# One-hot gate spreading in a transformer kernel: iota read from PSUM, low parts all on GpSimd, copies out of PSUM in 16-byte runs, one group of expert tiles fewer beside it

## The reference, cut to what matters

```python
idx = jnp.take_along_axis(cand_i..., best_pos, axis=-1)      # 8 heads x 16 experts per token
gate = jax.nn.softmax(best_s, axis=-1)
...
act = jax.nn.gelu(jnp.einsum('bpd,bphkd->bphk', hb, u_tab[ib]), approximate=False)
coef = (act * gb).astype(hb.dtype)
return jnp.einsum('bphk,bphkd->bpd', coef, v_tab[ib])
```

## Time and profile before

| | before |
|---|---|
| median of 3 runs | 2282.73 us (2278.05 to 2283.14) |
| profiled execution, its own time | 2281.69 us |
| span of the profiled execution | 2279.9 us |
| busy: PE, DVE, POOL, ACT | 2137.2, 1462.7, 1047.4, 926.5 us |
| mean granted clock of TensorE | 0.981 |

### The profile page before, as it was taken

The page is one execution under the profiler, slowest core; times in us unless marked ns, Lnnn a source line. Parts: engine busy times, 40 slices in busy tenths (PEclk is TensorE's granted clock), DMA queues, the critical chain, the costliest instruction groups (busy, mean ns, idle before and its releaser), DMA issues.

```text
span 2279.9 us, 27268 instructions
## 1 busy us (share of the span) xinstructions
PE 2137.2 (94%) x10296; PEld 1675.8 (74%) x10296; DVE 1462.7 (64%) x2308; ACT 926.5 (41%) x1527; POOL 1047.4 (46%) x828
## 2 busy tenths in 40 slices
PE   8999999999999999999999988787888699999999
PEld 6877767468787667878787766666666588888887
DVE  6456175442337742248989599999995366666665
ACT  4223354642333233013344466566664444433342
POOL 6555654304232217778588877777775300000000
PEclk9999999999999999999999999999999799999999
DMA  5221322202011112232166545556667688888884
GB/s 202 86 78 71 130 68 88 73 28 84 32 43 56 56 38 93 93 129 93 56 194 210 188 147 213 199 211 232 217 206 260 249 288 291 289 288 288 289 287 160
DMA packets 98291, 359.32 MB, mean 158 GB/s; under 512 B 8480, under 2 KB 41504, under 8 KB 73328
## 3 DMA queue, kind: packets, MB, share of 16 engines
q1 hardware_dynamic: 98160, 357.56, 45.4%
HBM read 286.09 MB, written 71.30 MB: 157 GB/s over the span
## 4 chain that ended last, share of the span: by engine, by line
PE 66%; DVE 18%; POOL 8%; issue 5%; ACT 3%; DMA 1%; SPq 0%; DVEq 0%; POOLq 0%; ACTq 0%
PE ps L1434 10%; PE ps L1435 10%; PE ps L797 9%; PE ps L798 9%; PE ps L799 9%; POOL wring_parts L2621 5%; DVE area L2505 2%; PE ps L1244 2%; PE ps L786 2%; PE ps L1381 2%; PE ps L1382 2%; DVE area L2489 2%; DVE area L2408 2%; DVE area L2490 2%; DVE area L2405 1%
## 5 line engine op out<-in xcount | busy, mean ns | idle before, releaser
L1381 PE MATMUL ps<-sqbuf_parts,wring_parts 128*128 128x512 f32 x1024 | 423.4, 413 | 23.7 <-POOL wring_parts L2621 23.7
L2621 POOL TENSOR_TENSOR wring_parts<-wring_parts,wring 128x512 fp32r<-128x512 f32 x256 | 380.8, 1515 | 136.9 <-ACT wring_parts L1852 136.9
L2577 POOL CAST wring_parts<-wring 128x512 fp32r<-128x512 f32 x236 | 169.6, 759 | 546.1 <-PE ps L799 429.1
L1382 PE MATMUL ps<-normed_x_parts,wring_parts 128*128 128x512 f32 x1024 | 413.8, 404 | 0.0
L2581 POOL TENSOR_TENSOR wring_parts<-wring,wring_parts 128x512 fp32r<-128x512 f32 x244 | 351.4, 1471 | 6.6 <-ACT wring_parts L1848 1.5
L1381 PEld LDWEIGHTS ps<-sqbuf_parts,wring_parts 128*128 128x128 f32 x1024 | 200.7, 196 | 70.8 <-POOL wring_parts L2621 23.4
L1382 PEld LDWEIGHTS ps<-normed_x_parts,wring_parts 128*128 128x128 f32 x1024 | 200.1, 195 | 43.3
L1884 ACT ACTIVATE area<-area,rt 128x128 bf16<-128x128 bf16 x512 | 162.6, 390 | 135.2 <-DVE area L2489 135.2
L797 PE MATMUL ps<-resid_parts,wring_parts 128*128 128x512 f32 (+1 forms) x528 | 201.9, 382 | 6.2 <-DVE normed_x_parts L2005 3.3
L798 PE MATMUL ps<-normed_x_parts,wring_parts 128*128 128x512 f32 (+1 forms) x528 | 197.6, 374 | 0.0
L799 PE MATMUL ps<-resid_parts,wring_parts 128*128 128x512 f32 (+1 forms) x528 | 196.8, 373 | 0.0
(11 more groups left out here) (269 smaller groups left out, 4546.9 us busy)
## 6 DMA issues: line engine op xcount, KB each, us to landing
wring<-in_weights_dram SPq DMA_DIRECT2D x65, 1024.0 KB, 4.8
wring<-in_uT_dram SPq DMA_DIRECT2D x128, 512.0 KB, 4.2
area<-in_vT_dram SPq DMA_DIRECT2D x44, 1024.0 KB, 6.7
hidden_table<-area SPq DMA_DIRECT2D x32, 1024.0 KB, 6.5
gate_table<-area SPq DMA_DIRECT2D x32, 1024.0 KB, 7.5
area<-gate_table SPq DMA_DIRECT2D x32, 1024.0 KB, 9.0
wring<-in_vT_dram SPq DMA_DIRECT2D x20, 1024.0 KB, 6.9
rt<-hidden_table SPq DMA_DIRECT2D x32, 512.0 KB, 4.6
```

What stands on the lines that cost most here:

```text
L1381: pe.matmul(out, first[:, d], h_first[:, k, :], start=(k == 0), stop=False)
L1382: mm = pe.matmul(out, rest[:, d], h_rest[:, k, :], start=False, stop=(k == KD - 1))
L2577: ins = nc.gpsimd.tensor_copy(up[:, d, :], W(name)[:, d, :])
L2621: ins = nc.gpsimd.tensor_tensor(rest[:, a:a + PIECE], first[:, a:a + PIECE], u_raw[t % len(USLOT)][:, a:a + PIECE], ALU.subtract)
```

## The change

Five things are done, all in the quads' part and around it.

1. ScalarE copies `iota` once into PSUM bank 7 (`iota_ps`). VectorE reads it there for both one-hots, in place of SBUF. The quads' matmuls have three banks in place of four.
2. All 128 low products go to GpSimd (`low_gates`). VectorE makes none.
3. Quads are prepared three ahead (`LEAD` = 3) in place of two.
4. The copy out of PSUM runs over experts outside and four tokens inside. It writes runs of 4 numbers (16 bytes), 256 bytes apart, and reads PSUM in steps of 512 bytes.
5. `BESIDE` is 17, so the quads end at tile 111. In SyncE's queue a part of a piece is stored ahead of the point where new ones are queued, what is left is stored at tile 112, and the first loads of the combination move to tile 121, behind the last `load_u`.

```diff
-BEFORE, BESIDE = 11, 18
+BEFORE, BESIDE = 11, 17
+LEAD = 3
+        iota_ps = ps[:, 7, 0:P]
         def spread_out(n):
-            return ps[:, 4 + n % 4, :].rearrange("p (t n) -> p t n", t=4)
+            return ps[:, 4 + n % 3, :].rearrange("p (t n) -> p t n", t=4)
...
+                if parts:
+                    store_piece(*parts.pop(0))
                 for n in quads_at(g, j):
                     if (n + 1) % (QUADS // PIECES) == 0:
                         parts += [(n // (QUADS // PIECES), part) for part in range(STORES)]
-                if parts and (n != QUADS - 1 or not quads_at(g, j)):
-                    store_piece(*parts.pop(0))
-                if t == EG * (BEFORE + BESIDE) - 1:
+                if t == EG * (BEFORE + BESIDE):
                     while parts:
                         store_piece(*parts.pop(0))
+                if t == TILES - len(USLOT) - 1:
                     sp.wait_ge(stored[0], 8 * PIECES * STORES)
                     load_v(0)
...
-                if n % 2:
-                    pe.wait_ge(odd_low, n // 2 + 1)
-                if n >= 4:
-                    pe.wait_ge(copied, n - 3)
+                pe.wait_ge(gates_low, n + 1)
+                if n >= 3:
+                    pe.wait_ge(copied, n - 2)
...
+            act.activation(iota_ps, C("iota"), ACT.Copy).then_inc(places_copied, 1)
             act.wait_ge(gates_split, 1)
-            weigh_gates(0)
-            weigh_gates(1)
+            for n in range(LEAD):
+                weigh_gates(n)
...
-                iota = C("iota").unsqueeze(1).to_broadcast([P, 4, P])
+                iota = iota_ps.unsqueeze(1).to_broadcast([P, 4, P])
                 dve.tensor_tensor(oneB[:, q], iota, across(1), ALU.is_equal).then_inc(hot_second, 1)
-                ins = dve.tensor_tensor(oneA[:, q], iota, across(0), ALU.is_equal)
-                if n % 2:
-                    ins.then_inc(hot, 1)
-                    return
-                dve.wait_ge(hot_second, n + 1)
-                dve.tensor_tensor(gateB[:, q, :, 1, :], oneB[:, q], w_lo[:, tokens]...to_broadcast([P, 4, P]),
-                                  ALU.mult).then_inc(hot, 1)
+                dve.tensor_tensor(oneA[:, q], iota, across(0), ALU.is_equal).then_inc(hot, 1)
...
-                dst = stage[:, piece % 2, :].rearrange("p (j t) -> p t j", t=HALF)
+                dst = stage[:, piece % 2, :].rearrange("p (j t) -> p j t", t=HALF)
                 dve.wait_ge(spread, n + 1)
-                dve.tensor_copy(dst[:, 4 * i:4 * i + 4, :], spread_out(n)).then_inc(copied, 1)
+                dve.tensor_copy(dst[:, :, 4 * i:4 * i + 4], spread_out(n).rearrange("p t n -> p n t")).then_inc(copied, 1)
...
-            for t in range(split + 1, TILES):
-                split_u(t)
+            for t in range(split + 1, TILES + 4):
+                if t < TILES:
+                    split_u(t)
                 if t == EG * BEFORE + 3:
                     pool.wait_ge(gates_split, 1)
-                    low_of_odd(1)
-                if t >= 4:
-                    for n in quads_at((t - 4) // EG, (t - 4) % EG):
-                        if n % 2 and n + 2 < QUADS:
-                            low_of_odd(n + 2)
+                    for n in range(LEAD):
+                        low_gates(n)
+                for n in quads_at((t - 4) // EG, (t - 4) % EG):
+                    if n + LEAD < QUADS:
+                        low_gates(n + LEAD)
```

More of the change, by code:

```diff
@@ L535, in build @@
         hot_gates = sem("hot_gates")
-        odd_low = sem("odd_low")
+        gates_low = sem("gates_low")
+        places_copied = sem("places_copied")
         gates_rounded = sem("gates_rounded")
@@ L1918, in _ @@
                     for n in quads_at(g, j):
-                        if n + 2 < QUADS:
-                            weigh_gates(n + 2)
+                        if n + LEAD < QUADS:
+                            weigh_gates(n + LEAD)
             for g in range(BEFORE + BESIDE, GROUPS):
@@ L2489, in one_hots @@
                 dve.tensor_tensor(oneB[:, q], iota, across(1), ALU.is_equal).then_inc(hot_second, 1)
-                ins = dve.tensor_tensor(oneA[:, q], iota, across(0), ALU.is_equal)
-                if n % 2:
-                    ins.then_inc(hot, 1)
-                    return
-                dve.wait_ge(hot_second, n + 1)
-                dve.tensor_tensor(gateB[:, q, :, 1, :], oneB[:, q], w_lo[:, tokens].unsqueeze(2).to_broadcast([P, 4, P]),
-                                  ALU.mult).then_inc(hot, 1)
+                dve.tensor_tensor(oneA[:, q], iota, across(0), ALU.is_equal).then_inc(hot, 1)
             def add_quad(n):
@@ L2532, in _ @@
             dve.tensor_tensor(w_lo, entT[:, 2, :], w_hi, ALU.subtract).then_inc(gates_split, 1)
-            for n in range(2):
+            dve.wait_ge(places_copied, 1)
+            for n in range(LEAD):
                 one_hots(n)
             for n in range(QUADS):
-                if n + 2 < QUADS:
-                    one_hots(n + 2)
+                if n + LEAD < QUADS:
+                    one_hots(n + LEAD)
                 add_quad(n)
@@ L2635, in _, with low_gates @@
                         split_u(split)
-            def low_of_odd(n):
+            def low_gates(n):
                 pool.wait_ge(hot_second, n + 1)
@@ L2642, in low_of_odd @@
                 w = w_lo[:, 4 * n:4 * n + 4].unsqueeze(2).to_broadcast([P, 4, P])
-                nc.gpsimd.tensor_tensor(gateB[:, n % 4, :, 1, :], oneB[:, n % 4], w, ALU.mult).then_inc(odd_low, 1)
-            for t in range(split + 1, TILES):
-                split_u(t)
+                nc.gpsimd.tensor_tensor(gateB[:, n % 4, :, 1, :], oneB[:, n % 4], w, ALU.mult).then_inc(gates_low, 1)
+            for t in range(split + 1, TILES + 4):
+                if t < TILES:
+                    split_u(t)
                 if t == EG * BEFORE + 3:
                     pool.wait_ge(gates_split, 1)
-                    low_of_odd(1)
-                if t >= 4:
-                    for n in quads_at((t - 4) // EG, (t - 4) % EG):
-                        if n % 2 and n + 2 < QUADS:
-                            low_of_odd(n + 2)
+                    for n in range(LEAD):
+                        low_gates(n)
+                for n in quads_at((t - 4) // EG, (t - 4) % EG):
+                    if n + LEAD < QUADS:
+                        low_gates(n + LEAD)
 def at_least(eng, s, value):
```

## The result

The changed kernel takes 2180.9 us (median of 4 runs, 2178.3 to 2182.5) against 2282.8 us: 0.956 of the time, interval 0.954 to 0.957. The profiled execution has a span of 2176.5 us.

What follows compares the result with a forecast made beforehand. VectorE bounds the quads now, GpSimd afterwards: 1310 + 353 + 1 + 8 = 1672 us, then 59.4 us of tiles puts tile 127's gelu at 1731.6, 73 us earlier; 2281.7 - 73 gives 2209 us, range 2195 to 2254.

Steps and rivals of the forecast that it cites:

- the price of the low product: GpSimd's low products in the quads' stretch: 1.45 us each from start to start, as before the change, at least 1.36.
- GpSimd would be the bound at 353 us: Quads' stretch: 128 low products of 1.45 us and 67 splits of 2.50 us make GpSimd the slowest engine.
- The loop: Quads' stretch, low product, quad, tile, gelu, rounding, split: 10.2 us for two tiles against 10.8 of GpSimd's work.
- the rival that named the loop: The loop over TensorE, ScalarE and GpSimd rules the quads' stretch: about 2225 us, chance 0.12.
- Two of its signs: Changed profile: GpSimd without waits for ScalarE from about 1315 to 1665 us; TensorE waiting for GpSimd's low products, not VectorE.
- The one-hots from PSUM: VectorE's 256 one-hots with iota in PSUM: 0.60 us each from start to start, the short form.
- the split at 2.50: GpSimd's split of a tile beside the quads falls to 2.50 us, with 3.30 kept for the range.
- The tail: Tiles 112 to 127 behind the quads: 59.4 us without the old 21 us stall; a stall staying had chance 0.08.
- the lower of the two bounds: VectorE's copy out of PSUM: 0.60 us if neither write nor read steps cost, 0.90 if the read costs.
- The rival on the other side: PSUM reads in 512-byte steps make VectorE's copy the bound: about 2308 us at 2.4 us a copy, chance 0.07.
- the 8 us allowed: Quads' stretch: 8 us, between 0 and 18, added for TensorE's granted clock staying below full.
- Its low end: The range's 2195 us: low products of 1.36 us and no loss to the clock.

## Why the prediction was wrong

**The step that failed** is the price of the low product: "One takes 1.49 us there, 1.45 from start to start; I keep that, since it does not show the spread that the split shows, and 1.36 is the least I would allow." It takes 1.04 us, 1.00 from start to start. All 64 of them had been stretched before, so no spread showed. The split's rows had given the surcharge: 1.73 us against 1.25. The low product's 1.49 against 1.04 is the same 0.45, and with `iota` back in SBUF it returned (1.48). A duration from the old state was carried into a new state for one instruction and not for its neighbour on the same engine. On 128 low products it is 58 us of GpSimd. With it failed what was built on it, that GpSimd would be the bound at 353 us.

**What that did.** GpSimd needs 128 x 1.00 + 67 x 2.50 = 296 us, not 353, and is not the bound. The loop, worked out at 10.17 us for two tiles, becomes 9.72 us with the smaller low product; 9.84 was measured. Lead and order of the low products moved it as it should (10.83 and TensorE's own pace). So the rival that named the loop had the mechanism, at a price that was too high because of the same term. The quads ended at 1642 us and not at 1672, and this is the 30 us by which the profiled execution lay below its forecast (2178.3 us against 2208.7; the median lies 28 below 2209). Two of its signs failed with it: GpSimd was to have no waits for ScalarE and had 34, and TensorE was to wait for low products and did so for only 10.6 us.

**Right.** The one-hots from PSUM at 0.60 us from start to start, and the split at 2.50: both as taken, and they carry the change (71 us alone, 85 us lost without). VectorE's need was 128 x 1.80 = 230 us. The Trainium skill's rule (SBUF — State Buffer, Who interferes with whom) held: one SBUF input, no contention (0.68 us with GpSimd at work). The Trainium skill says too (SBUF — State Buffer, Summary: rules for kernel authors) that the second to issue fully blocks until the first has finished. That fits VectorE, whose one-hot took 2.28 us behind a GpSimd instruction of 2.93. It fits GpSimd's surcharge of 0.45 us, which is about the rest of a VectorE instruction under way: with `iota` in PSUM alone all 14 stretched low products start 0.13 to 0.17 us behind a VectorE instruction with two SBUF inputs, and none of the other 50 does. No run moves that start by itself, so this rests on rows that coincide and not on an edit.

**The tail** came out at 59.6 us from the last copy's end to tile 127's gelu, as forecast, but with less room: ScalarE waited 6.55 us for a load of `u` until 1663.6 us, where the prediction had named no such wait. TensorE did not stop for it; the gelus at 1656.4 and 1671.3 us are four tiles apart, 3.73 us each. Undoing it costs 14.5 us.

**The copy** was 0.69 us, the lower of the two bounds, and irrelevant to the time, as the sum had it. The rival on the other side, a dear strided read, had no substance. The clock took less than the 8 us allowed: 0.98 in the stretch in place of 0.95, with TensorE stopping less.

The range was too narrow below. Its low end was also summed wrong: by its own terms, 128 x 0.09 = 11.5 us for low products and 8 us for the clock off 2209, it is 2189 us and not 2195. The 2180.9 lie below that too, for one reason: the low end allowed 1.36 us for the low product, the shortest in the profile of before, and a one-hot of VectorE ran beside that one too.

## What to carry to other kernels

When a change takes a contention away, every instruction on both engines has to be priced at its undisturbed duration, the unmoved ones too. An instruction that shows only one duration may always have been disturbed; a sister instruction on the same engine that shows two tells the surcharge. When one engine's work falls, work out the loops over engines before adding up each engine: here VectorE, ScalarE and GpSimd each had room (236.5, 254.3 and 298.9 of 333 us), and order and lead of 1 us instructions were worth 19 and 33 us.

## What the runs showed of the hardware

A GpSimd subtraction or product that starts just behind a VectorE instruction with two SBUF inputs pays some 0.45 to 0.55 us once, whatever its length: 1.04 to 1.49 us, 1.25 to 1.73, 2.40 to 2.93. The VectorE instruction then stays at 0.68 to 0.75 us. One that starts behind GpSimd's waits for it (1.01 us behind a low product, 1.75 behind a split's half, 2.28 behind the long one), and GpSimd's keeps its length if it starts first (1.05 us). With one VectorE input in PSUM neither is lengthened: 0.68 us beside 1.04 and 1.30. VectorE's copy from PSUM takes 1.06 us for 512 numbers written 256 bytes apart and 0.69 us as soon as two neighbours are written together; reading PSUM in steps of 512 bytes costs nothing that shows, since a contiguous copy of 528 took 0.70 us.
